# Softmax factors of a hybrid attention layer turned and repeated by transfers through device memory

## The reference

```
s   = q @ k.T * scale - slope[h] * dist
p   = masked_softmax(s)                      # exp(s - max) / sum
o_h = p @ v                                  # per head h, (tokens, 64)
o_nsa = g[...,0:1]*o_cmp + g[...,1:2]*o_slc + g[...,2:3]*o_win
```

## Time and profile before

| | us |
|---|---|
| median of 3 runs | 748.39 (748.23 to 749.61) |
| profiled execution | 748.56 |
| its span in the profile | 746.8 |
| busy: TensorE, VectorE, ScalarE, GpSimd | 737.7, 525.4, 416.6, 178.8 |

### The profile page before, as it was taken

How to read it: one execution, slowest core, us unless ns; L and a number is a source line. 1 busy time by engine, 2 the same in 40 slices (tenths; PEclk the granted TensorE clock), 3 DMA queues, 4 the chain that set the end, 5 groups by cost and what they waited for, 6 DMA issues and landing times.

```text
span 746.8 us, 11968 instructions
## 1 busy us (share of the span) xinstructions
PE 737.7 (99%) x4398; PEld 642.0 (86%) x4398; DVE 525.4 (70%) x999; ACT 416.6 (56%) x777; POOL 178.8 (24%) x192
## 2 busy tenths in 40 slices
PE   9999999999999999999999999999999999999998
PEld 9988977877997878777888899999998888888886
DVE  5478888779986977757668988988887544434443
ACT  7768377756678886664356565565565323232230
POOL 3110346424555553300023323222220000000000
PEclk9999999999999999999999999999999999999999
DMA  9622222111111021112632333333333232333322
GB/s 334 248 80 68 62 82 81 33 31 56 57 57 57 29 86 29 57 57 84 203 108 85 90 109 113 114 107 94 102 96 112 86 111 87 99 99 89 109 84 113
DMA packets 21833, 70.95 MB, mean 95 GB/s; under 512 B 2448, under 2 KB 3600, under 8 KB 21520
## 3 DMA queue, kind: packets, MB, share of 16 engines
q1 hardware_dynamic: 21776, 70.19, 30.2%
HBM read 68.08 MB, written 2.10 MB: 94 GB/s over the span
## 4 chain that ended last, share of the span: by engine, by line
PE 83%; DVE 8%; ACT 5%; issue 2%; DMA 2%; POOL 0%; SPq 0%; DVEq 0%
PE psum L1830 23%; PE psum L1832 23%; PE psum L1831 23%; PE psum L1838 5%; PE psum L2027 4%; PE psum L2004 2%; PE psum L2005 2%; DMA x2T<-in_xT 1%; DVE w_lo L1311 1%; ACT w_hi L929 1%; DVE x2T L1812 1%; DVE prob L1525 1%; ACT h L929 1%; ACT q_st L929 1%; DVE x2T L1678 1%
## 5 line engine op out<-in xcount | busy, mean ns | idle before, releaser
L929 ACT ACTIVATE w_hi<-stage 128x512 fp32r<-128x512 f32 (+4 forms) x149 | 118.3, 802 | 113.5 <-DMA stage<-in_panels 107.3
L1311 DVE TENSOR_TENSOR w_lo<-stage,w_hi 128x1024 fp32r<-128x1024 f32 (+4 forms) x74 | 76.4, 1037 | 110.1 <-ACT w_hi L929 105.8
L1830 PE MATMUL psum<-hT_hi,w_hi 128*128 128x256 f32 (+1 forms) x324 | 113.5, 350 | 1.0 <-DVE q_st L1467 0.6
L1831 PE MATMUL psum<-hT_lo,w_hi 128*128 128x256 f32 (+1 forms) x324 | 107.3, 331 | 0.0
L1830 PE MATMUL psum<-a_hi,w_hi 128*128 128x512 f32 x256 | 99.7, 389 | 0.2 <-issue 0.2
L1832 PE MATMUL psum<-a_hi,w_lo 128*128 128x512 f32 x256 | 99.6, 389 | 0.0
L1831 PE MATMUL psum<-a_lo,w_hi 128*128 128x512 f32 x256 | 99.6, 389 | 0.0
L1832 PE MATMUL psum<-hT_hi,w_lo 128*128 128x512 f32 (+1 forms) x264 | 90.6, 343 | 0.0
L1116 ACT ACTIVATE prob<-prob,neg_max 128x128 f32<-128x128 f32 (+3 forms) x96 | 53.8, 560 | 34.5 <-DVE neg_max L1525 33.8
L893 POOL TENSOR_TENSOR w_lo<-stage,w_hi 128x512 fp32r<-128x512 f32 x46 | 59.8, 1304 | 36.7 <-ACT w_hi L929 36.7
L1830 PE MATMUL psum<-t_hi,w_hi 128*128 128x256 f32 x240 | 67.9, 283 | 0.0
(11 more groups left out here) (276 smaller groups left out, 1708.9 us busy)
## 6 DMA issues: line engine op xcount, KB each, us to landing
stage<-in_panels SPq DMA_DIRECT2D x104, 512.0 KB, 3.6
xT_in<-in_xT SPq DMA_DIRECT2D x8, 260.0 KB, 4.9
x_in<-in_x SPq DMA_DIRECT2D x4, 512.0 KB, 7.1
phi<-in_phi SPq DMA_DIRECT2D x2, 1024.0 KB, 6.4
x2T<-in_xT SPq DMA_DIRECT2D x1, 2048.0 KB, 9.2
out_xT<-x2T SPq DMA_DIRECT2D x8, 256.0 KB, 2.0
stage<-in_panels SPq DMA_DIRECT2D x8, 212.0 KB, 4.9
stage<-in_panels SPq DMA_DIRECT2D x4, 408.0 KB, 3.1
```

The costliest lines, as they stand in the source:

```text
L929: return nc.scalar.activation(dst, src, ACT.Copy, scale=scale)
L1311: tt_op(w_lo[:, p % SLOTS, cols], stage[:, p % SLOTS, cols], hi_place(p)[:, cols].bitcast(F32), ALU.subtract)\
L1830: mm(dst, a_h, b_h, start=start, stop=False)
L1831: mm(dst, a_h, b_l, start=False, stop=False)
```

## The change

The factor takes another way for tiles 0 to 10; tile 11 keeps the old one. Step inv at 8ti+9: GpSimd writes only the 128x8 values of inverse sum times gate into `fac_n` (two buffers, ordered as head parity, then pair). Step fac_out at 8ti+9 (late): ScalarE waits for them and issues a transfer that writes them turned, as [8 heads, 128 tokens] of single 4-byte elements, to `fac_rows` in device memory. Step fac_in at 8ti+11 (late): ScalarE waits until that transfer has landed and the close before is done, and issues two transfers that each read four heads' rows (2 KB in one piece) into 64 partitions of `fac`. VectorE's close waits for both. TAKEN_AT grows by 2, so close comes at unit 8ti+14. The bank of the O ring that cmpS, cmpPT, cmpO, kc, kcT, kwT, qaT and fac use is computed from TAKEN_AT, so some of these (qaT at units 53 and 62 for instance) use the other bank.

```diff
-    TAKEN_AT = H + PV_LAG
+    TAKEN_AT = H + PV_LAG + 2
...
-    for ti in range(NU // H):
+
+    LAST = NU // H - 1
+    for ti in range(LAST):
         at_unit(ti * H + 9, "inv", ti, at=early)
-        at_unit(ti * H + 10, "fac", ti)
+        at_unit(ti * H + 9, "fac_out", ti)
+        at_unit(ti * H + 11, "fac_in", ti)
+    at_unit(LAST * H + 9, "inv", LAST, at=early)
+    at_unit(LAST * H + 10, "fac", LAST)
...
+        fac_n = place_small("fac_n", [P, 2, H])
...
+        fac_rows = nc.dram_tensor("fac_rows", (LAST, H, P), F32, kind="Internal").ap()
...
                     pool.wait_ge(inv_done, ti + 1)
-                    if ti:
+                    inv = row_inv[:, ti * H:(ti + 1) * H]
+                    if ti >= 2:
+                        pool.wait_ge(fac_left, 16 * (ti - 1))
+                    dst = fac_n[:, ti % 2, :].rearrange("p (a k) -> p k a", a=2)
+                    if ti == LAST:
                         wait_drained(pool, ("O", ti - 1))
-                    inv = row_inv[:, ti * H:(ti + 1) * H, None].to_broadcast([P, H, DH])
-                    dst = fac[:, :, :].rearrange("p k (a d) -> p (k a) d", d=DH)
-                    if br == DSA:
-                        nc.gpsimd.tensor_copy(dst, inv).then_inc(fac_spread, 1)
+                        dst = fac[:, :, :].rearrange("p k (a d) -> p (k a) d", d=DH)
+                        nc.gpsimd.tensor_copy(dst, inv[:, :, None].to_broadcast([P, H, DH])).then_inc(fac_spread, 1)
+                    elif br == DSA:
+                        nc.gpsimd.tensor_copy(dst, inv.rearrange("p (k a) -> p k a", a=2)).then_inc(fac_spread, 1)
                     else:
-                        nc.gpsimd.tensor_tensor(dst, inv, gates[:, tt, :, 1 + br, None].to_broadcast([P, H, DH]),
-                                                ALU.mult).then_inc(fac_spread, 1)
+                        gate = gates[:, tt, :, 1 + br].rearrange("p (k a) -> p k a", a=2)
+                        nc.gpsimd.tensor_tensor(dst, inv.rearrange("p (k a) -> p k a", a=2), gate, ALU.mult)\
+                            .then_inc(fac_spread, 1)
...
+                elif kind == "fac_out":
+                    ti, = a
+                    se.wait_ge(fac_spread, ti + 1)
+                    nc.scalar.dma_start(fac_rows[ti].rearrange("h t -> t h"), fac_n[:, ti % 2, :],
+                                        allow_slow_non_contiguous=True).then_inc(fac_left, 16)
+                elif kind == "fac_in":
+                    ti, = a
+                    se.wait_ge(fac_left, 16 * (ti + 1))
+                    if ti:
+                        wait_drained(se, ("O", ti - 1))
+                    for i in range(2):
+                        src = fac_rows[ti, i * 4:(i + 1) * 4].rearrange("k t -> (k t)")[None, :].to_broadcast([DH, 4 * P])
+                        nc.scalar.dma_start(fac[i * DH:(i + 1) * DH, :, :].rearrange("p k t -> p (k t)"), src)\
+                            .then_inc(fac_loaded, 16)
...
                 elif kind == "close":
                     ti, = a
                     br, tt, _ = units[ti * H]
-                    wait_drained(ve, ("fac", ti))
+                    if ti == LAST:
+                        wait_drained(ve, ("fac", ti))
+                    else:
+                        ve.wait_ge(fac_loaded, 32 * (ti + 1))
```

More of the change, by code:

```diff
@@ L604, in hybrid_layer @@
         fac_spread = sem("fac_spread")
+        fac_left = sem("fac_left")
+        fac_loaded = sem("fac_loaded")
         oT_hi_done = sem("oT_hi_done")
```

## The result

The changed kernel takes 797.29 us (median of 4 runs, 795.52 to 798.3) against 748.31 us (748.09 to 749.61) before: a ratio of 1.0647, 95% interval 1.0634 to 1.066. It is 49 us slower, where 743.8 was forecast. The direction is that of rival B, whose price was +4.9 us: a tenth of it.

What follows compares the result with a forecast made beforehand. TensorE was taken to set the unit loop's pace. Transposes -4.8, waits -0.7, ScalarE's transfers +0.5 and +0.4 for transposes behind VectorE waits gave -4.6, so 748.39 became 743.8 us; range 742.0 to 750.5.

Steps and rivals of the forecast that it cites:

- rival B: Unit loop: the element-wise write lands late and the close waits; +4.9 us, 753.3 us; chance 0.18.
- What bounds the kernel: Unit loop: TensorE sets the pace, VectorE nearly does around 180 us, ScalarE has slack.
- rival A: Unit loop up to about 190 us: VectorE takes over, about half of 4.8 us is left; 746.0 us; chance 0.13.
- The removed work: Tiles 0 to 10: 44 TensorE transposes give 4.8 us, waits for GpSimd's spreading 0.7, less 0.4 behind VectorE waits.
- so I take 3.5: ScalarE's write of 1,024 4-byte elements: landing taken as 3.5 us, so its wait at unit 8ti+11 costs nothing.
- the upper bound of 9.2: Bound for the write's landing: the x2T load's 9.2 us for 1,024 rows of 2 KB.
- One unit of cover: Rival B, VectorE's late close: TensorE may run one set of scores ahead, hiding 2.3 us at tile 8.
- I add 2: Rival B: 2 us added for ScalarE's waits beyond one unit and the slack of a tile.
- The loads themselves: The two factor loads VectorE's close at 8ti+14 waits for: 2.0 us, 3.6 for the range; wait priced at nothing.
- the panels' wait: SP's panel loads share the DMA engines, busy 11 to 18%; the new 260 KB a tile are hidden.
- The moves: Close two units later, some small PSUM uses on the other O bank: nothing, at most one 0.7 us close.
- ScalarE's three issues: Three transfers a tile, 1.3 us replacing the copy's 0.59; mostly covered, 0.5 us charged from 250 to 270 us.

Runs made afterwards that it cites:

- no_turn: Kernel before without the four transposes and ScalarE's copy of tiles 0 to 10, nothing in their place: 743.55 us against 748.84, ratio 0.9924.
- w_apart: Changed kernel, qaT's bank at unit 62 put back, each of 1,024 elements written into its own 64 bytes, loads reading x: 744.85 us, ratio 0.9948.
- w_rows_bank: w_rows with qaT at unit 62 put back on the other O bank: 744.86 us, ratio 0.9947 to the kernel before.
- turn_small: Changed kernel, bank put back, factors turned by one 128x8 TensorE transpose, copied by ScalarE, written as 8 rows of 512 bytes: 747.98 us against 748.53 before.
- turn_blocks: Changed kernel, bank put back, factors turned on VectorE in 32x32 blocks, written as 128 rows of 128 bytes: 747.79 us against 748.88 before.
- w_rows: Changed kernel with the 4 KB written as 128 rows of 32 bytes, unturned, waits and loads kept: 749.05 us against 748.84 before, ratio 1.0000.

## Why the prediction was wrong

**What bounds the kernel** held: no_turn shows TensorE setting the pace, against rival A.

**The removed work** held: 5.1 us forecast, 5.3 measured; priced at start-to-start 0.44 us for four, not at the recorded 274 ns each, which would have given 12.

**The step that failed first** is "In pieces it is nearest to the latter, in bytes (4 KB) far below either", from which followed "so I take 3.5". The landing was 9.0 to 11.3 us where it could be read, in most tiles above the upper bound of 9.2. That bound was right in size by accident: x2T's time is data, this write's is neither data nor packets. I had thought about how many pieces move, not about where they land; 1,024 pieces 64 bytes apart land in 3.0 us (w_apart). The Trainium skill ("DMA: Bandwidth & Descriptors", Rules for kernel authors) warns against this pattern, and with the changed kernel's addresses this case agrees, at 49 us; w_apart writes one by one too and costs nothing that shows in the time, so its reason, taken alone, is not what made this write late.

**The second failure** is the cover in rival B. It had the right mechanism and put even a landing of 9.2 us at +4.9. One unit of cover on VectorE, and "I add 2" for ScalarE, assumed that the two waits hide separately. They come one behind the other: ScalarE stands 2.2 to 6.4 us until the write has landed and issues the loads only then, its probT copies come late and TensorE stands for them, and VectorE's close waits until the loads have landed too (37.3 us in all, much of it while TensorE stands as well). The loads themselves, taken at 2.0 us, landed after 3.5, and after 2.9 behind a prompt write. Of the 37.7 us that TensorE stood, 28.4 were for probT copies and 8.6 for VectorE's q_st (5.2 of them at the bank of tile 7), and TensorE's idle time grew by 36.6 us.

**Nor was the panels' wait there.** "SP's panel loads share the DMA engines ... the new 260 KB a tile are hidden" counted bytes. It was not bytes but the late write that stopped the panels: at tile 4 two landed after 12.4 us in place of 4.0, ScalarE waited 8.9 us for one, and TensorE 7.6 us (of its 28.4) behind ScalarE.

**Not in any case** was the clock: with the idle stretches the granted clock came down to 0.93 in the mean, and TensorE's busy time rose by 11.4 us with less work. The two parts, 36.6 of idling and 11.4 of slower work, make up the 48 us by which the loop's stretch is longer.

**The moves** were priced at "nothing, at most one 0.7 us close", and cost 4.5 us in the kernel before. The rule used (a close two units earlier is enough) looked at who frees the bank for qaT; it left out who needs it next. ScalarE's three issues, the loads and the late close together took 1.3 to 1.6 us (w_rows_bank, w_apart) where 0.5 was forecast: small, but about three times as much.

## What to carry to other kernels

Don't turn small data by writing single elements side by side into device memory: the landing of such a transfer isn't bounded by its packets, and other queues' transfers stand behind it. Turned on an engine, they cost nothing against before, but gained at most 1 us (turn_small, turn_blocks). Data spread out in device memory were written promptly, but no run reads them back. When a step moves, check for each buffer it rotates who waits for it next, not only who frees it. A wait on an in-order engine is to be costed as a chain through everything queued behind it, and on a TensorE-bound kernel with the clock on top.

## What the runs showed of the hardware

- 1,024 single 4-byte elements from SBUF into 4 KB of device memory: packets through 1.6 to 4.6 us after the issue (tile 0: 8 ns each), landing 9.0 to 11.3 us after it; 512 of them: 7.7 to 11.1 us; the same 1,024 at 64 bytes' distance: 3.0 us; 128 rows of 32 bytes: 1.4 us.
- Panel loads of 512 KB on another queue, issued behind such a write, landed 13.0 to 14.9 us after the write's issue; two issued together took 12.4 us in the median, in place of the 4.0 beside a prompt write (w_rows) and the 6.1 beside the spread one (w_apart).
- The issue doesn't grow with the pieces: 0.37 us for 1,024 elements, 0.33 us for 128 rows.
- With waits of up to 7.6 us on TensorE, stretches of the loop ran at the lower clock level, although TensorE is busy 94% of the span.
- A transpose of 128x32 in f32 on VectorE in 32x32 blocks takes 0.21 us.
